# An eleventh weight place from halved attention maps, weight loads three places ahead, and a moved second-tile key projection

## The chip, the cores and the metric

One NeuronCore of a Trainium2 chip. The time is the device time of the kernel in microseconds, the median of the runs of one program.

## The reference, cut to what matters

A two-layer encoder over 256 tokens of width 1024, in float32, taken as two tiles of 128 tokens. For each layer `mix = token_mixers(h)`, then `h = layer_norm(a*h + mix)`, then the experts, then a gate:

```python
proj = h @ w_in                  # dq, dk, dv (differential attention), sq, sk, sv (sparse attention), iq, ik, iw (indexer)
w = a[:, 0] - lam * a[:, 1]      # 4 heads, two softmax maps each
_, sel = lax.top_k(iscore, 64)   # sparse attention: 8 heads, one map each, over the 64 chosen keys
q = (xt @ w_q).reshape(TOKEN_BLOCK, 8, 2, 128)           # PEER
s = jnp.einsum('thcd,hckd->thck', q, skf)                # top 16 of each half, top 16 of the 256 sums
act = jax.nn.gelu(jnp.einsum('thkd,td->thk', u_tab[eidx], xt))
out = jnp.einsum('thk,thkd->td', g * act, v_tab[eidx])   # 128 experts of a token
r = r + sigmoid(r @ ple_wg + ple_bg) * (p @ ple_wp)
```

Attention is causal in chunks of 64: tile 0 sees 128 keys, tile 1 sees 256.

## The kernel before

**Passes and pairs.** Each of the four (layer, tile) combinations is a pass: MIX[0..3] mixes the tokens and chooses experts, then 128 indirect gathers bring for each token one row of u and v (128 x 2048 float32, 1 MB a gather), then CLOSE[0..3] applies the gate. The gathers of a pass are worked off in 64 pairs, which make up a phase: phase 1 works off the experts of pass 0 and, woven in between the pairs, runs MIX[1]; phase 2 runs CLOSE[0] and MIX[2], phase 3 CLOSE[1] and MIX[3], phase 4 CLOSE[2] and the start of CLOSE[3]. Phase 0, ahead of them, has MIX[0] and the beginning of MIX[1] and no pairs.

**A pair.** GpSimd issues the gathers into a ring of 8 row slots (L622), each after TensorE has used the slot's former row. VectorE makes the dot product with the token (L1303), ScalarE the gelu and the scaled diagonal matrix `dg` (L832, L835), TensorE adds the weighted v rows into PSUM (`acc`, L1663, in the last pass L1658), which frees the two slots.

**Weights.** They come in blocks of 128 x 2048 (1 MB) from SyncE's queue (L571), strictly in the order in which TensorE uses them, into a `store` of 10 places; a load waits until the last reader of its place is done. `count_uses` gives each block the place that has been free longest. MIX[n] of tile 1 uses the weights of the same layer as MIX[n-1]: eight blocks (`KEPT_BLOCKS`: the sub-keys and all expert-query blocks but the first) stay in the store from tile 0 to tile 1. For MIX[1] six further blocks (`EARLY`: the index weights, dq0, dq1, dk0, dk1) are put by MIX[0] into ring slots 2 to 7, and the first gathers into those slots wait until MIX[1] has used them (the wait on `block_done` ahead of L622). dq1 stands for the second half of the differential-query weights, dk0 and dk1 for those of the keys, pq2a and pq2b for the expert queries of group 2, ps2 for their scores against the sub-keys.

**Order.** It is written out by hand. `START_PE`, `START_ACT`, `START_DVE` list phase 0 (a + marks parts of MIX[1]); `FIRST_PLAN`, `PROJECT_PLAN`, `ATTEND_PLAN`, `CLOSE_PLAN` give for each part the pair ahead of which TensorE, ScalarE and VectorE run it; `attend_first` and `attend_last` shift the plan in phases 1 and 3, `behind_close` in phase 2. `SINGLY_FIRST` and `SINGLY_PROJECT` place the projections of MIX[1] and MIX[3] one block a pair. The selection of experts is in steps A (top 16 of the two halves), B (top 16 of the sums) and C (looking up the indices) for five groups of heads: A2a is step A of group 2, first head. They run on VectorE (`choose`, from L1227), with an exponential on ScalarE (L777) in step C.

**Maps.** `ex` (128 x 8 x 256) holds the eight exponential maps of either attention, then the key scores of all 16 expert lists and the lookup's one-hot rows; `probsT` (128 x 16 x 128) their transposes, the expert queries, and the gains and shifts of the closing norm. The part `wts0`/`wts1` combines the two differential maps (from L993); `spt0`, `spt1` and `spv` transpose the sparse maps and multiply them with the values (L1480).

## Time and profile before

| | |
|---|---|
| median of 3 runs | 1598.83 us (1597.42 to 1599.74) |
| profiled execution, its own time | 1597.55 us |
| span of its instructions | 1595.8 us |
| TensorE, VectorE, ScalarE, GpSimd busy | 76%, 66%, 42%, 36% |
| moved | 648.45 MB, 406 GB/s over the span |
| indirect gathers | 510, median 16.0 us from issue to landing |
| weight loads of 1 MB into the store | 93, median about 10 us from issue to landing |
| chain that ended last | DMA 45%, TensorE 30%, VectorE 14%, ScalarE 7% |

How to read it: the page cuts the span into 40 slices of 39.9 us and gives for each the busy tenths of each engine and the GB/s moved; a window view gives the same for stretches one names. A wait is put down to the instruction that came last among those waited for. Times of single instructions come from the timeline view, which merges neighbours of one line.

### The profile page before, as it was taken

Reading aid. Unit: us, or ns where it says so; the run is one execution under the profiler, and the core shown is the slowest. Engines: PE = TensorE matmul, PEld = TensorE weight load, DVE = VectorE, ACT = ScalarE, POOL = GpSimd, SP = SyncE. Lnnn points to the kernel's source line nnn. Section 1 sums busy time; section 2 is a strip of 40 time slices with the busy share of each in tenths; the row PEclk is TensorE's granted clock in tenths of the full one; section 3 lists DMA queues with packets and bytes.
Section 4 is the critical chain, followed back from the end, with each engine's and each line's share of the span. In section 5 each row is a group of like instructions: output and inputs, shape, how many; then the busy total and the mean of one; then the engine's idle time right before and its main releaser. Section 6 shows DMA issues by size and latency. Waiting matters only on the chain.

```text
span 1595.8 us, 22703 instructions
## 1 busy us (share of the span) xinstructions
PE 1213.1 (76%) x8234; PEld 603.9 (38%) x8234; DVE 1045.3 (66%) x2636; ACT 668.6 (42%) x2027; POOL 580.9 (36%) x518
## 2 busy tenths in 40 slices
PE   9999868787868689786895977978798768444556
PEld 9686423333532266231551335524255223000112
DVE  3467997745778664654688684575578958644555
ACT  2323445723344435363344532536344534323444
POOL 0013443443333323343344332334443434544441
PEclk9999989898888899797997978999899876555557
DMA  9869999999999999999999999999999999999996
GB/s 384 360 250 396 396 421 420 421 421 420 421 420 421 417 396 421 421 420 421 421 421 421 421 417 370 420 421 420 422 420 419 420 421 420 422 421 421 421 421 248
DMA packets 91344, 648.45 MB, mean 406 GB/s; under 512 B 10144, under 2 KB 11616, under 8 KB 13152
## 3 DMA queue, kind: packets, MB, share of 16 engines
q0 software_dynamic: 74016, 536.90, 81.3%
q1 hardware_dynamic: 16704, 109.76, 16.8%
q8 instruction: 65, 1.06, 0.3%
q10 hardware_dynamic: 512, 0.34, 0.1%
q14 instruction: 47, 0.39, 0.1%
HBM read 645.91 MB, written 1.05 MB: 405 GB/s over the span
## 4 chain that ended last, share of the span: by engine, by line
DMA 45%; PE 30%; DVE 14%; ACT 7%; issue 3%; POOL 2%; SPq 0%; ACTq 0%; DVEq 0%; POOLq 0%
DMA rows<-uv_dram,rows_of 39%; PE bank L1343 10%; PE acc L1663 7%; DVE rows L1303 7%; PE bank L1361 5%; DMA store<-wmix_dram 4%; POOL rows L622 2%; ACT dg L835 1%; PE acc L1658 1%; ACT L832 1%; ACT ex L748 1%; PE bank L1614 1%; DMA rows<-wmix_dram 1%; ACT gel L832 1%; DMA store<-wclose_dram 1%
## 5 line engine op out<-in xcount | busy, mean ns | idle before, releaser
L622 POOL DMA_INDIRECT rows<-uv_dram,rows_of x510 | 576.7, 1131 | 985.9 <-PE acc L1663 661.3
L1303 DVE CUSTOM_DVE_ANT_0 rows<-rows,hb 128x1024 f32<-128x1024 f32 x384 | 463.9, 1224 | 313.1 <-DMA rows<-uv_dram,rows_of 310.6
L1663 PE MATMUL acc<-rows,dg 64*64 64x512 f32 x3072 | 453.1, 701 | 198.0 <-ACT dg L835 196.2
L832 ACT ACTIVATE gel<-dots 128x1 f32<-128x1 f32 x512 | 102.7, 201 | 630.1 <-DVE dots L1303 628.7
L1663 PEld LDWEIGHTS acc<-rows,dg 64*64 64x64 f32 x3072 | 102.0, 145 | 459.7 <-ACT dg L835 369.3
L1343 PE MATMUL bank<-xT,store 128*128 128x128 f32 x1888 | 235.1, 286 | 15.7 <-DMA store<-wmix_dram 10.4
L1343 PEld LDWEIGHTS bank<-xT,store 128*128 128x128 f32 x1888 | 225.5, 200 | 55.5 <-issue 41.9
L1303 DVE CUSTOM_DVE_ANT_0 rows<-rows,store 128x1024 f32<-128x1024 f32 x128 | 155.5, 1224 | 119.3 <-DMA rows<-uv_dram,rows_of 118.7
L1658 PE MATMUL acc<-rows,dg 128*32 128x256 f32 x1024 | 119.7, 565 | 133.3 <-ACT dg L835 132.8
L835 ACT ACTIVATE dg<-dg,gel 128x64 f32<-128x64 f32 (+1 forms) x512 | 174.7, 341 | 48.4 <-ACT gel L832 1.5
L1361 PE MATMUL bank<-store,xT 128*128 128x512 f32 x352 | 166.3, 618 | 17.2 <-DMA store<-wmix_dram 14.4
L829 ACT ACTIVATE dg<-fixed,g_of 128x64 f32<-128x64 f32 (+1 forms) x512 | 143.5, 329 | 1.4 <-ACT probsT L648 0.3
L1658 PEld LDWEIGHTS acc<-rows,dg 128*32 128x32 f32 x1024 | 25.9, 132 | 222.9 <-ACT dg L835 212.5
L1361 PEld LDWEIGHTS bank<-store,xT 128*128 128x128 f32 x352 | 66.3, 196 | 110.4 <-issue 94.0
L832 ACT ACT_TABLE_LOAD x51 | 65.4, 1283 | 0.9
L648 ACT ACTIVATE probsT<-bank 128x512 f32<-128x512 f32 (+1 forms) x59 | 30.7, 545 | 42.4 <-PE bank L1343 32.6
L1303 DVE DVE_READ_ACCUMULATOR2_ANT dots<- 128x1 f32 x512 | 42.1, 82 | 0.0
L648 ACT ACTIVATE qT<-bank 128x512 f32<-128x512 f32 (+1 forms) x18 | 9.9, 550 | 59.7 <-PE bank L1343 49.8
L1489 PE MATMUL bank<-prm,fixed 64*128 64x256 f32 x96 | 27.5, 433 | 0.0
L777 ACT ACT_TABLE_LOAD x20 | 25.7, 1283 | 0.4
L1253 DVE TENSOR_TENSOR ex<-ex,i16f 128x512 f32<-128x512 f32 (+1 forms) x38 | 22.6, 594 | 1.3
L1256 DVE TENSOR_REDUCE sel<-ex 128x32 f32<-128x512 f32 (+1 forms) x38 | 22.4, 588 | 1.3
(230 smaller groups left out, 1016.2 us busy)
## 6 DMA issues: line engine op xcount, KB each, us to landing
store<-wmix_dram SPq DMA_DIRECT2D x78, 1024.0 KB, 9.7
store<-wclose_dram SPq DMA_DIRECT2D x15, 1024.0 KB, 10.4
rows<-uv_dram,rows_of POOLq DMA_INDIRECT x510, 16.0
rows<-wmix_dram SPq DMA_DIRECT2D x5, 1024.0 KB, 14.8
...
```

The source lines that it names most:

```text
L622: pool.indirect_dma_start(out=rows[:, slot, :], out_offset=None, in_=uv_d[phase // TILES], in_offset=bass.IndirectOffsetOnAxis(ap=rows_of[ ...
L648: ins = A(out, src, func)
L777: A(gexp[:, 0:gs], gexp[:, 0:gs], ACT.Exp).then_inc(gexp_ready, 1)
L829: A(dg[:, s + j, 0:w], one, ACT.Identity, scale=g_of[:, phase % 2, col:col + 1]).then_inc(diag_ready, 1)
L832: A(gel[:, s + j:s + j + 1], dots[:, s + j:s + j + 1], ACT.Gelu).then_inc(gelu_done, 1)
L835: A(dg[:, s + j, 0:w], dg[:, s + j, 0:w], ACT.Identity, scale=gel[:, s + j:s + j + 1]).then_inc(dg_ready, 1)
L1303: V.tensor_tensor_reduce(out=rows[:, s, 0:D], in0=rows[:, s, 0:D], in1=tokens, scale=1.0, scalar=0.0, op0=ALU.mult, op1=ALU.add, accum_out ...
L1343: ins = MM(bk[:, T * at:T * at + T], w[:, T * c:T * c + T], src[:, c, :], start=(c == 0), stop=(c == KC - 1))
L1361: ins = MM(bk[:], xT[:, 2 * q + c, :], w[:, 512 * c:512 * c + 512], start=(q == 0 and c == 0 and extra is None), stop=(q == 3 and c == 1), ...
L1489: ins = MM(bk[:, QCOLS * j:QCOLS * j + QCOLS], chooser(first + i // 2, 2 * (i % 2) + j), prm[:], start=True, stop=True)
L1658: ins = MM(quarters(acc, c)[BT * k:BT * k + BT, :], dg[:, s, 0:BT], rows[:, s, D + 256 * k:D + 256 * k + 256], start=False, stop=False, sk ...
L1663: ins = MM(acc[HT * j:HT * j + HT, 512 * r:512 * r + 512], dg[at, s, :], rows[at, s, D + 512 * j:D + 512 * j + 512], start=False, stop=Fal ...
```

## The change

- `ex` and `probsT` are halved. For tile 1 the eight maps go through in two halves of four: the second half's exponentials wait until the first half has been combined (differential) or transposed (sparse); `wts` and `spv` are split accordingly; the scores of groups 3 and 4 are copied once earlier groups are looked up. The gains and shifts of the closing norm lie half in `sc`.
- The store has 11 places.
- A block of MIX[1] and later takes the third newest of the free places; MIX[0]'s blocks take the oldest, as before. The places for the last pass's spread tokens are the three longest free then, no longer 0, 1 and 2.
- dk0 and dk1 of MIX[0] are loaded into the store and held there for MIX[1] (`LENT`), no longer into ring slots 6 and 7. MIX[1] runs them ahead of pairs 3 and 9 of phase 1, no longer in phase 0; the rest of its projections moves by four pairs.
- The selections of pass 0 in phase 1 and their queries are moved by one to three pairs, and `ATTEND_PLAN` by up to two, `attend_first` by up to two more.

```diff
@@ -46,7 +46,7 @@
-PLACES = 10
+PLACES = 11
...
+HELD = 4
...
@@ -157,7 +158,7 @@
-        blocks = [b for b in blocks if b not in EARLY]
+        blocks = [b for b in blocks if b not in EARLY + LENT]
...
@@ -169,23 +170,23 @@
...
-    ("exps0", None, 18, None), ("exps1", None, 19, None), ("dv0", 17, None, None), ("dv1", 18, 19, None),
+    ("exps0", None, 18, None), ("dv0", 17, None, None), ("dv1", 18, 19, None),
...
-    ("sel0", None, None, 20), ("wts0", None, None, 21), ("wts1", None, None, 22), ("sel1", None, None, 22),
+    ("wts0", None, None, 20), ("exps1", None, 21, None), ("sel0", None, None, 21), ("wts1", None, None, 22), ("sel1", None, None, 22),
...
-    ("sexp0", None, 26, None), ("sexp1", None, 27, None), ("rms", None, 28, 27), ("rms2", None, None, 29),
-    ("spt0", 27, 28, None), ("spt1", 28, 29, None), ("spv", 30, None, None), ("merge", None, None, 32),
-    ("gb0", 28, 29, None), ("gb1", 29, 30, None), ("mT0", 30, 31, None), ("mix0a", 32, None, None),
-    ("mT1", 33, 34, None), ("mix1a", 33, None, None), ("mix0b", 34, None, None), ("mix1b", 35, None, None),
+    ("sexp0", None, 26, None), ("rms", None, 28, 27), ("rms2", None, None, 29),
+    ("spt0", 27, 28, None), ("sexp1", None, 28, None), ("gb0", 28, 29, None), ("spv0", 29, None, None), ("spt1", 30, 31, None),
+    ("gb1", 31, 32, None), ("mT0", 31, 32, None), ("spv1", 32, None, None), ("mix0a", 33, None, None), ("mix1a", 34, None, None),
+    ("merge", None, None, 34), ("mT1", 35, 36, None), ("mix0b", 36, None, None), ("mix1b", 37, None, None),
...
-    ("B1a", None, None, 49), ("perm0", 49, None, 51), ("pq3b", 49, 50, None), ("C1a", None, 51, 50), ("ps3", 50, 51, None),
+    ("B1a", None, None, 49), ("perm0", 49, None, 51), ("pq3b", 49, 50, None), ("C1a", None, 51, 50), ("ps3", 51, 53, None),
...
-    ("A2a", None, None, 53), ("A2b", None, None, 54), ("ps4", 54, 55, None), ("B2a", None, None, 56), ("B2b", None, None, 57),
-    ("C2a", None, 59, 58), ("C2b", None, None, 60), ("perm2", 61, None, 63), ("A3a", None, None, 61), ("A3b", None, None, 62),
+    ("A2a", None, None, 53), ("A2b", None, None, 54), ("B2a", None, None, 56), ("B2b", None, None, 57),
+    ("C2a", None, 59, 58), ("ps4", 58, 61, None), ("C2b", None, None, 60), ("perm2", 61, None, 63), ("A3a", None, None, 61), ("A3b", None, None, 62),
...
@@ -220,20 +221,20 @@
-START_PE = ("wake T idx dq0 dq1 dk0 dk1 iw ds0 ix sq0 sq1 dv0 dv1 dpt sk0 dpv sk1 ss0 sv0 sv1 mT0 mix0a spt0 spt1 mix1p spv mix1a mT1 "
-            "T1+ mix0b mix1b idxa+ h1T pq0a ps0 idxb+ dq0+ pq1a init ps1 dq1+ dk0+ dk1+").split()
+START_PE = ("wake T idx dq0 dq1 dk0 dk1 iw ds0 ix sq0 sq1 dv0 dv1 dpt sk0 dpv sk1 ss0 sv0 sv1 mT0 mix0a spt0 spt1 mix1p spv0 spv1 mix1a mT1 "
+            "T1+ mix0b mix1b idxa+ h1T pq0a ps0 idxb+ dq0+ pq1a init ps1 dq1+").split()
...
-    ("pq2a", 0, None, None), ("pq2b", 1, 2, None), ("pq3a", 2, None, None), ("ps2", 3, 4, None), ("pq3b", 4, 5, None),
-    ("pq4a", 5, None, None), ("ps3", 6, 7, None), ("pq4b", 7, 8, None), ("ps4", 9, 10, None),
+    ("pq2a", 1, None, None), ("pq2b", 2, 3, None), ("ps2", 4, 5, None), ("pq3a", 5, None, None), ("pq3b", 7, 8, None),
+    ("ps3", 8, 9, None), ("pq4a", 10, None, None), ("pq4b", 11, 12, None), ("ps4", 13, 14, None),
...
-    ("A2a", None, None, 4), ("A2b", None, None, 5), ("B2a", None, None, 6), ("B2b", None, None, 7), ("C2a", None, 9, 8),
-    ("C2b", None, None, 9), ("perm2", 9, None, 11), ("A3a", None, None, 11), ("A3b", None, None, 12), ("B3a", None, None, 13),
-    ("B3b", None, None, 14), ("C3a", None, 16, 15), ("C3b", None, None, 16), ("perm3", 17, None, 19), ("A4a", None, None, 17),
-    ("A4b", None, None, 18), ("B4a", None, None, 19), ("B4b", None, None, 20), ("C4a", None, 22, 21), ("C4b", None, None, 22),
-    ("perm4", 23, None, 25),
+    ("A2a", None, None, 5), ("A2b", None, None, 6), ("B2a", None, None, 7), ("B2b", None, None, 8), ("C2a", None, 10, 9),
+    ("C2b", None, None, 10), ("perm2", 10, None, 12), ("A3a", None, None, 12), ("A3b", None, None, 13), ("B3a", None, None, 14),
+    ("B3b", None, None, 16), ("C3a", None, 18, 17), ("C3b", None, None, 18), ("perm3", 18, None, 20), ("A4a", None, None, 19),
+    ("A4b", None, None, 20), ("B4a", None, None, 21), ("B4b", None, None, 23), ("C4a", None, 25, 24), ("C4b", None, None, 25),
+    ("perm4", 26, None, 28),
...
@@ -242,8 +243,18 @@
     ("dk0", 16, None, None), ("dk1", 17, 18, None), ("iw", 18, 19, None), ("sq0", 18, None, None), ("sq1", 19, 20, None),
 ]
 SINGLY_FIRST = [
-    ("T", 9, 10, None), ("par", 9, 10, None), ("sq0", 11, None, None), ("iw", 13, 14, None), ("sq1", 13, 14, None),
+    ("dk0", 3, None, None), ("dk1", 9, 10, None), ("T", 13, 14, None), ("par", 13, 14, None), ("sq0", 15, None, None),
+    ("iw", 17, 18, None), ("sq1", 17, 18, None),
 ]
+def behind_mix(row):
...
+    part, *pairs = row
+    late = [p for p in pairs if p is not None]
+    if part[:2] in ("sp", "gb", "mT", "mi", "me") or min(late) < 37:
+        return row
+    return (part, *(None if p is None else p + (2 if p < 54 else 1 if p < 62 else 0) for p in pairs))
...
 SINGLY = {"dv0": (18, None, None), "dv1": (19, 20, None), "sv0": (20, None, None), "sv1": (21, 22, None)}
...
@@ -257,12 +268,15 @@
...
 def attend_first(p):
...
-    return p + max(0, min(6, 6 - (p - 50) // 3))
+    return p + max(0, min(8, 8 - (p - 50) // 3))
...
+ATTEND_PLAN = [behind_mix(row) for row in ATTEND_PLAN]
...
 def make_plan():
@@ -270,7 +284,6 @@
-    plan["ACT"][1].append((1, "dk1", MIX[1]))
...
@@ -318,18 +331,18 @@
...
-EARLY = [(U_IQ, U_IQ + 1), (U_IK,)] + [tuple(units_of(part)) for part in ("dq0", "dq1", "dk0", "dk1")]
-EARLY_SLOTS = (3, 2, 4, 5, 6, 7)
+EARLY = [(U_IQ, U_IQ + 1), (U_IK,)] + [tuple(units_of(part)) for part in ("dq0", "dq1")]
+EARLY_SLOTS = (3, 2, 4, 5)
+LENT = [tuple(units_of(part)) for part in ("dk0", "dk1")]
...
-HX_BLOCKS, SPREAD_BLOCK = 2, 2
-HELD_LATE = (0, 1, SPREAD_BLOCK)
+AHEAD = 3
...
-    if run is MIX[1] and block in EARLY:
+    if run is MIX[1] and block in EARLY + LENT:
...
@@ -348,7 +361,7 @@
...
-    uses, free = [0] * PLACES, [-1] * PLACES
+    uses, free, late = [0] * PLACES, [-1] * PLACES, ()
...
@@ -357,8 +370,10 @@
             if run is MIX[0] and block in EARLY:
                 place = (PLACES + EARLY.index(block), 0)
             else:
-                at = min((a for a in range(PLACES) if run is not CLOSE[2] or a not in HELD_LATE), key=lambda a: free[a])
-                assert free[at] < i
+                if run is CLOSE[2] and not late:
+                    late = tuple(sorted(range(PLACES), key=lambda a: free[a])[:3])
+                open_to = sorted((a for a in range(PLACES) if free[a] < i and a not in late), key=lambda a: free[a])
+                at = open_to[0] if run is MIX[0] else open_to[max(0, len(open_to) - AHEAD)]
                 place = (at, uses[at])
                 uses[at] += 1
                 free[at] = end if run is CLOSE[2] else last[run.key, block]
@@ -369,11 +384,12 @@
...
-    return bank, unit, uses
+    return bank, unit, late, uses
...
-BANK, UNIT, USES = count_uses()
+BANK, UNIT, HELD_LATE, USES = count_uses()
+SPREAD_BLOCK = HELD_LATE[0]
...
@@ -416,8 +431,8 @@
-        ex = sb("ex", [128, 8, SEQ])
-        probsT = sb("probsT", [128, 16, T])
+        ex = sb("ex", [128, HELD, SEQ])
+        probsT = sb("probsT", [128, 2 * HELD, T])
...
@@ -500,6 +519,16 @@
+        def map_of(run, i):
...
+            i = i % HELD if run.tile else i
+            return ex[:].rearrange("p a k -> p (a k)")[:, run.keys * i:run.keys * i + run.keys]
...
+        def halves_of(h0, nh):
...
+            at = 2 * (h0 % HELD)
+            return slice(at, at + 2 * nh)
...
@@ -732,8 +763,10 @@
                 if part in ("exps0", "exps1"):
...
+                    if half and tile:
+                        act.wait_ge(dw_ready, DIFF_HEADS * n + DIFF_HEADS // 2)
...
-                        A(ex[:, i, 0:run.keys], sc[:, i, 0:run.keys], ACT.Exp, bias=nmx[:, i:i + 1], scale=SCALE,
+                        A(map_of(run, i), sc[:, i, 0:run.keys], ACT.Exp, bias=nmx[:, i:i + 1], scale=SCALE,
...
@@ -744,12 +777,14 @@
                 if part in ("sexp0", "sexp1"):
...
+                    if half and tile:
+                        act.wait_ge(*full_at(run, "spt1"))
...
-                        A(ex[:, i, 0:run.keys], sc[:, i, 0:run.keys], ACT.Exp, bias=snmx[:, i:i + 1], scale=SCALE,
+                        A(map_of(run, i), sc[:, i, 0:run.keys], ACT.Exp, bias=snmx[:, i:i + 1], scale=SCALE,
...
-                        take(run, name, quarter(probsT, int(name[3])))
+                        take(run, name, quarter(probsT, int(name[3]) % 2))
...
@@ -769,7 +804,9 @@
...
-                    take(run, part[:3], lists[:, 2 * h0:2 * h0 + 2 * nh, :].rearrange("p c t -> p (c t)"), slice(0, 2 * nh * T))
+                    if part in ("ps3", "ps4"):
+                        act.wait_ge(*((rows_picked, len(GROUPS) * n + g - 1) if n < LAST else (chosen_ready, g - 1)))
+                    take(run, part[:3], lists[:, halves_of(h0, nh), :].rearrange("p c t -> p (c t)"), slice(0, 2 * nh * T))
...
@@ -990,24 +1027,26 @@
...
+                    half = int(part[3])
+                    if half == 0:
...
+                    maps = slice(4 * half, 4 * half + 4)
+                    dve.wait_ge(dexp_ready, 8 * n + 4 * half + 4)
...
@@ -1466,20 +1506,23 @@
...
+                if part in ("spv0", "spv1"):
...
-                    bk, full = bank(run, "spv")
...
+                    bk, full = bank(run, "spv") if half == 0 else opened(run, "spv")
...
+                            ins = MM(bk[:, DH * hd:DH * hd + DH], probsT[:, ((tile + 1) * hd + k) % (2 * HELD), :],
...
```

## Rows read from the trace of the kernel before

**Rows 1.** The page: its head, the 40 slices' rate, the packets.

```profile
span 1595.8 us, 22703 instructions
...
GB/s 384 360 250 396 396 421 420 421 421 420 421 420 421 417 396 421 421 420 421 421 421 421 421 417 370 420 421 420 422 420 419 420 421 420 422 421 421 421 421 248
DMA packets 91344, 648.45 MB, mean 406 GB/s; under 512 B 10144, under 2 KB 11616, under 8 KB 13152
```

**Rows 2.** Windows: length, PE, PEld, DVE, ACT, POOL busy, granted clock, DMA share, GB/s.

```profile
70.00:105.00 35.00, 33.56 (x210) 25.40 (x209) 12.54 (x45) 5.38 (x12) 2.12 (x2) 1.00 0.50 170
105.00:115.00 10.00, 10.00 (x89) 9.07 (x88) 9.16 (x37) 5.15 (x11) 3.89 (x5) 1.00 0.95 368
...
125.00:145.00 20.00, 19.86 (x167) 13.53 (x166) 12.36 (x44) 9.66 (x26) 7.69 (x9) 1.00 0.97 370
...
160.00:175.00 15.00, 11.60 (x89) 4.70 (x87) 14.55 (x40) 10.45 (x29) 8.05 (x7) 0.96 0.93 350
175.00:550.00 375.00, 283.80 (x1728) 129.06 (x1724) 271.23 (x712) 162.14 (x484) 139.99 (x126) 0.88 1.01 421
550.00:585.00 35.00, 25.32 (x167) 13.60 (x168) 31.26 (x70) 16.30 (x46) 11.82 (x11) 0.80 0.99 386
...
950.00:970.00 20.00, 12.02 (x93) 9.09 (x93) 15.91 (x37) 9.83 (x28) 5.30 (x4) 0.81 1.00 408
970.00:985.00 15.00, 15.00 (x122) 11.91 (x123) 4.93 (x8) 3.31 (x13) 4.79 (x4) 0.91 0.75 289
```

**Rows 3.** SyncE's timeline, 90 to 100 and 175 to 185: start, length.

```profile
96.49 0.33 SPq L571 DMA_DIRECT2D store<-wmix_dram  x1
...
180.33 0.33 SPq L571 DMA_DIRECT2D store<-wmix_dram  x1
```

**Rows 4.** TensorE's timeline, 96 to 130.

```profile
108.08 10.88 PE L1343 MATMUL bank<-res,rows 128*128 128x128 f32 x96
118.80 3.74 PE L1343 MATMUL bank<-xT,store 128*128 128x128 f32 x32
122.46 1.95 PE L1663 MATMUL acc<-rows,dg 64*64 64x512 f32 x16
```

**Rows 5.** GpSimd's timeline, 100 to 130: in brackets idle before, releaser.

```profile
112.09 0.93 POOL L622 DMA_INDIRECT rows<-uv_dram,rows_of  x1 [3.22 <-PE bank L1343]
...
119.23 0.93 POOL L622 DMA_INDIRECT rows<-uv_dram,rows_of  x1 [2.64 <-PE bank L1343]
124.36 0.94 POOL L622 DMA_INDIRECT rows<-uv_dram,rows_of  x1 [4.20 <-PE acc L1663]
```

**Rows 6.** ScalarE's and VectorE's timelines, 112 to 132.

```profile
115.06 0.35 ACT L835 ACTIVATE dg<-dg,gel 128x64 f32<-128x64 f32 x1
...
120.61 1.22 DVE L1303 CUSTOM_DVE_ANT_0 rows<-rows,hb 128x1024 f32<-128x1024 f32 x1
...
130.37 0.17 DVE L1278 TENSOR_REDUCE gsum<-gexp 128x1 f32<-128x16 f32 x1 [7.07 <-ACT gexp L777]
```

**Rows 7.** TensorE's timeline, 950 to 980.

```profile
957.47 1.95 PE L1663 MATMUL acc<-rows,dg 64*64 64x512 f32 x16
967.40 6.31 PE L1343 MATMUL bank<-xT,store 128*128 128x128 f32 x32 [7.98 <-DMA store<-wmix_dram]
973.65 1.95 PE L1663 MATMUL acc<-rows,dg 64*64 64x512 f32 x16
```

**Rows 8.** SyncE's timeline, 955 to 958.

```profile
957.57 0.80 SPq L571 DMA_DIRECT2D store<-wmix_dram  x2
```

**Rows 9.** TensorE's timeline, 574 to 592.

```profile
574.46 5.62 PE L1343 MATMUL bank<-xT,store 128*128 128x128 f32 x48 [1.36 <-ACT xT L648]
...
581.89 7.41 PE L1343 MATMUL bank<-xT,store 128*128 128x128 f32 x64
```

**Rows 10.** The chain of waits at 337, and the window 335 to 350 around it.

```profile
337.62 10.24 DMA store<-wmix_dram
...
335.00:350.00 15.00, 12.12 (x52) 4.32 (x51) 4.93 (x8) 3.73 (x15) 3.75 (x4) 1.00 1.02 422
```

More of the change, by code:

```diff
@@ L811, in spread_out @@
                 for half, name in enumerate(banks_of(run, f"hx{c}")):
-                    take(run, name, hx[:, c, 512 * half:512 * half + 512])
+                    take(run, name, hx_of(c)[:, 512 * half:512 * half + 512])
                 for name in banks_of(run, f"hx{c}"):
@@ L992, in part_of @@
                     ins.then_inc(iscore_ready, 1)
[L993 to L995 removed]
+                if part in ("wts0", "wts1"):
+                    half = int(part[3])
+                    if half == 0:
+                        dve.wait_ge(lamexp_ready, n + 1)
+                        V.tensor_tensor(lamw[:, 4:5], lamw[:, 3:4], lamw[:, 2:3], ALU.subtract).then_inc(L.sem, L.one())
+                        settle()
+                        V.tensor_scalar(lamw[:, 5:6], lamw[:, 4:5], -LAM_INIT[run.layer], None, ALU.add).then_inc(L.sem, L.one())
+                    maps = slice(4 * half, 4 * half + 4)
+                    dve.wait_ge(dexp_ready, 8 * n + 4 * half + 4)
+                    V.reciprocal(rden[:, maps], den[:, maps]).then_inc(L.sem, L.one())
@@ L996, in part_of @@
                     settle()
-                    V.tensor_scalar(lamw[:, 5:6], lamw[:, 4:5], -LAM_INIT[run.layer], None, ALU.add).then_inc(L.sem, L.one())
-                    dve.wait_ge(dexp_ready, 8 * (n + 1))
-                    V.reciprocal(rden[:], den[:]).then_inc(L.sem, L.one())
+                    V.tensor_scalar(nmx[:, maps], rden[:, maps], lamw[:, 5:6], None, ALU.mult).then_inc(L.sem, L.one())
                     settle()
-                    V.tensor_scalar(nmx[:], rden[:], lamw[:, 5:6], None, ALU.mult).then_inc(L.sem, L.one())
+                    for hd in (2 * half, 2 * half + 1):
+                        V.tensor_scalar(map_of(run, 2 * hd + 1), map_of(run, 2 * hd + 1), nmx[:, 2 * hd + 1:2 * hd + 2],
+                                        None, ALU.mult).then_inc(L.sem, L.one())
@@ L1002, in part_of @@
                     settle()
-                    for hd in range(DIFF_HEADS):
-                        V.tensor_scalar(ex[:, 2 * hd + 1, 0:nk], ex[:, 2 * hd + 1, 0:nk], nmx[:, 2 * hd + 1:2 * hd + 2],
-                                        None, ALU.mult).then_inc(L.sem, L.one())
-                if part == "wts1":
-                    settle()
-                    for hd in range(DIFF_HEADS):
-                        V.scalar_tensor_tensor(sc[:, hd, 0:nk], ex[:, 2 * hd, 0:nk], rden[:, 2 * hd:2 * hd + 1],
-                                               ex[:, 2 * hd + 1, 0:nk], ALU.mult, ALU.add).then_inc(dw_ready, 1)
+                    for hd in (2 * half, 2 * half + 1):
+                        V.scalar_tensor_tensor(sc[:, hd, 0:nk], map_of(run, 2 * hd), rden[:, 2 * hd:2 * hd + 1],
+                                               map_of(run, 2 * hd + 1), ALU.mult, ALU.add).then_inc(dw_ready, 1)
```

42 lines of the change are left out of this document (22 added, 20 removed).

## The prediction

> **What bounds the kernel now.** The page comes first [rows 1]. The program moves 648.45 MB; its best slices move 420 to 422 GB/s and most slices stand there. At 421 GB/s that is 1540.2 us of a span of 1595.8 us, so the 16 DMA engines are the bound and only some 55 us are theirs to lose. TensorE (76%) and VectorE (66%) matter only where they keep a transfer from being asked for. So I read the trace as a list of holes: in a stretch of T us at g GB/s, T x (1 - g/421) us are lost. The windows [rows 2] give 20.9 us in 70 to 105; 1.3 in 105 to 115; 2.4 in 125 to 145; 2.5 in 160 to 175; 2.9 in 550 to 585; 0.6 + 4.7 in 950 to 985; most of the rest lies in the first 70 us and in the tail. Between 175 and 550 the rate is 421, as in nearly all later slices. An edit that neither closes nor opens a hole moves nothing: bytes are the same before and after the change.
>
> Then each hole's cause. *70 to 105*: no expert is chosen before 102.6 us, so only weights can move, and the places for them are full: SyncE issues a load at 96.49 and none again until 180.33 [rows 3]. *125 to 145*: TensorE runs six blocks of column weights (three of them, dq1, dk0 and dk1 of the second tile, in the 10.88 us row, then pq2a) before the first pair at 122.46 [rows 4]. The gathers into row slots 5, 6 and 7 wait one by one for dq1, dk0 and dk1, and the one into slot 0 again for that pair [rows 5]; VectorE meanwhile waits 7.07 us for an exponential which ScalarE makes only behind the copies of dk1 and pq2b [rows 6]. *970 to 985*: TensorE ends a pair at 959.4 and the next at 975.6, 16.2 us later, since dq0 was still under way [rows 7]. Its load and dq1's were issued from 957.57 on, within 0.8 us [rows 8], once the index weights were used: eight of the ten places hold weights kept for this tile, two circulate. The eight row slots are 8 x 2.49 = 19.9 us of transfer (1 MB at 421 GB/s), half of it spent when the stall began, so the engines ran dry at 970.
>
> **The change, part by part.** *The loan of dk0 and dk1.* Rows slots 6 and 7 are free for gathers at once; of eleven places the loan holds two, so nine circulate up to the first gather where ten did. One load fewer is under way before 105: 1 MB, 2.5 us more of the first hole. **Lost: 2.5.**
>
> *dk0 and dk1 behind pairs 2 and 8, pq2a behind pair 0.* The first pair no longer waits for 10.88 x 2/3 + 3.7 = 10.9 us of TensorE; its factors are there by 115.4 [rows 6], so it ends near 117.3 instead of 124.4, and slots 0 and 1 are asked for then. The gathers of slots 6 and 7 go out right behind slot 5's (112.09, 0.94 us each and a short gap), the last near 114.6 against 119.23. By 117.3, 9 MB are asked for and some 5 moved (3.7 in 105 to 115, and 2.3 us at the full rate), so about 10 us are in hand, until 127; pair 1 has its dot products at 121.8 [rows 6] and ends near 124.5, still inside. The copy of pq2b moves behind the exponential, so most of the 7.07 us goes. The hole of 125 to 145 closes: **2.4 gained**. That of 105 to 115 stays (it is the latency of the first gathers and slot 5's wait for dq1, which nothing moves).
>
> *Selections spread.* The same VectorE work, with more pairs that carry none (3, 4, 11, 15, 22; before only 3 and 10). In 160 to 175 VectorE is busy 14.55 of 15 us: the slots come free late because of it. With the 7 us from above in hand, and with two weight loads (behind dk0 and dk1) that now fall into a stretch without any [rows 3], I take 2.0 of the 2.5. **Gained: 2.0** (bounds 0 and 2.5).
>
> *Eleventh place in the fourth pass.* Three places circulate: the index weights and dq0 are there before the index part. dq1 and dk0 then take the two loads of 957.57, land near 967.3 [rows 7, 8] and dq1 is wanted at about 965.2 (957.5 + pair 1.95 + block 3.8 + pair 1.95). A wait of 2.1 us instead of 9.8, with two more gathers asked for at 965. The 5.3 us of 950 to 985 shrink to the 0.6 that VectorE causes. **Gained: 4.7** (bounds 2.4, half, and 5.3).
>
> *Loads three places ahead.* A load now goes into the third newest free place, not the oldest. In the first pass the oldest is still taken, and in the second and fourth only three places circulate anyway, so it bites in the third, where up to ten loads ran ahead. There TensorE is in one piece from 574 to 643: index part, pair, two blocks (7.4 us), pair, at 9.3 us a pair [rows 9]. dq1's load is issued when the first index block is done, at about 578.3, and wanted at 585.7; if it takes 9.8 us like that of rows 7, TensorE waits 2.4 us there. The hole that opens is bounded by nothing (337.62: a wait of 10.24 us for a load, at 422 GB/s all the while [rows 10]) and by that of rows 7 (4.7). The engines are at 386 GB/s just before, thus with little queued, and I take 1.2, the lower quarter. **Lost: 1.2.**
>
> *Halved maps.* The second half of the exponentials waits for the first half's weights or transposes, each placed a pair or more earlier on its engine; ps3 and ps4 copies wait for a lookup one pair back. Queued behind each such wait on ScalarE are the diagonals of the next pair, for which TensorE waits. The cover is the eight-deep ring; if it were gone, one wait would cost a pair, 5 us. The split products add two reciprocals and two small products a pass, each like the 0.17 us row of rows 6, under transfers. The rest of the mixer moves two pairs later; its first choices stand two pairs ahead of the gather that reads them, even in the pass where they are latest. **Nothing.**
>
> Sum against the profiled execution, 1597.55 us (span 1595.8 and 1.75 around it): -2.5 + 2.4 + 2.0 + 4.7 - 1.2 = 5.4 gained, 1592.15. The median shown is 1598.83, 1.28 above that execution, so for a median 1598.83 - 5.4 = **1593.4**.
>
> **The rivals.** *(a) More closes.* If no wait in the third pass opens a hole, and its 550 to 585 hole (2.9, VectorE busy 31.26 of 35 us) is filled since loads that ran ahead now come later: 2.4 + 2.5 + 5.3 + 2.9 + 1.3 - 2.5 = 11.9, 1586.9. For it, lost time is where loads are missing; against, a load still starts only when a block is used, and none is used there.
>
> *(b) The loads set the pace.* In rows 8 two loads, 2 MB, with gathers outstanding, took 9.8 us until TensorE went on: one MB per 4.9 us, while TensorE uses one per 4.65 in the third pass (9.3 a pair). Ten loads in hand hide that; three don't. At 2 x 4.98 = 9.96 us a pair, seven pairs last 4.6 us longer; if that reaches the end, 5.4 - 4.6 = 0.8 gained, 1598.0. Against: while TensorE waits, loads and gathers keep the engines at 421. The Trainium skill's page DMA: Bandwidth & Descriptors (Queues, rings and completion order) has each DMA engine take turns between the queue rows that have work; by that rule loads get half of the rate while gathers are queued, and the sum would be this 1598.0. Rows 8 fit it.
>
> *(c) Slower: starved third pass.* If three of its seven double blocks find a load late enough that two pair ends stand over 16.2 us apart (the gap of rows 7, from which a hole opened), each costs 4.7: 14.1 lost against 5.4 + 1.2 gained, 1598.83 + 7.5 = 1606.3. For: lead falls from ten loads to three in the densest stretch. Against: it takes 7 us of lateness on top of 9.3, three times, with three loads outstanding; rows 10 show ten us of lateness for nothing.
>
> *(d) The place is eaten by the loan.* The start gains nothing (0 of 2.0, 1.0 of 2.4) and the fourth pass half: -2.5 + 1.0 + 2.4 - 1.2 = -0.3, 1599.1.
>
> **How the numbers follow.** Forecast 0.60, (a) 0.13, (b) 0.07, (c) 0.10, (d) 0.10. A measurement of this kernel can tell about 0.2%, 3.2 us, from no change. Faster: forecast nearly whole (0.58) and (a) 0.13, 0.71. Same: (b), (d) and the forecast's upper edge, 0.18. Slower: (c) and 0.01 for sizes, 0.11. The range runs from (a) 1586.5 to 1600, past (b) and (d); outside are (c) and a twentieth beyond the ends. The bounds of the unknown terms (2.0, 2.3 and 3.5 downwards, 0.5, 0.6 and 1.2 upwards) lie within it but for all bad ones at once.
>
> **What would show it.** Right: first pair's matmuls near 115 and row slot 0 asked for again near 117; 125 to 145 and 160 to 175 at 415 GB/s or more; 70 to 105 poorer, near 140 GB/s; no DMA wait of TensorE over 3 us after the last pass's index part and no slice there at 370; a wait of 2 to 3 us for dq1 in the third pass. Wrong: new slices under 410 in the third pass (c), a VectorE hole that moved rather than closed, or 70 to 105 unchanged.

## The result, and the profile after

The kernel after takes 1600.39 us (median of 20 runs, 1597.35 to 1605.05) against 1597.66 us (20 runs, 1595.52 to 1600.56) of the kernel before on the same chip: a ratio of 1.0016, interval [1.0009, 1.0023]. It is slower by 2.7 us. That is less than the 0.2% that the prediction called tellable, but the interval leaves out a ratio of 1. The forecast was 5.4 us faster. The profiled execution of after took 1601.31 us.

The page of after: its head, the rate in the 40 slices, the packets.

```profile
span 1599.5 us, 22715 instructions
...
GB/s 385 333 255 421 420 421 405 421 421 421 421 420 389 403 407 420 421 421 422 421 420 421 421 420 420 421 421 409 421 421 394 387 421 420 422 421 421 421 421 248
DMA packets 91344, 648.45 MB, mean 405 GB/s; under 512 B 10144, under 2 KB 11616, under 8 KB 13152
```

Against [rows 1] the same bytes moved. The slices 4, 5 and 25 (396, 396, 370 before) now stand at 421, 420 and 420. New weak slices are the 7th, 13th, 14th, 28th, 31st and 32nd. The windows of after, first the stretches of [rows 2], then those that are new (columns as there):

```profile
0.00:70.00 70.00, 64.94 (x453) 54.25 (x454) 30.16 (x110) 21.60 (x59) 0.20 (x4) 1.00 0.97 390
70.00:105.00 35.00, 33.56 (x210) 25.56 (x209) 12.70 (x46) 5.38 (x12) 2.17 (x2) 1.00 0.44 162
105.00:115.00 10.00, 6.89 (x62) 5.76 (x64) 9.15 (x37) 5.15 (x11) 5.26 (x7) 1.00 0.97 380
125.00:145.00 20.00, 18.81 (x158) 12.41 (x156) 14.77 (x49) 8.05 (x27) 7.65 (x8) 1.00 1.01 420
160.00:175.00 15.00, 15.00 (x132) 11.91 (x135) 11.37 (x27) 7.57 (x21) 5.73 (x6) 1.00 1.01 418
250.00:265.00 15.00, 15.00 (x97) 10.21 (x95) 12.97 (x30) 6.08 (x18) 5.26 (x4) 0.89 0.98 378
485.00:500.00 15.00, 15.00 (x56) 5.58 (x55) 14.41 (x36) 5.19 (x15) 3.48 (x4) 0.87 0.85 332
550.00:585.00 35.00, 31.85 (x252) 23.78 (x252) 19.88 (x40) 11.82 (x37) 9.04 (x8) 0.95 0.99 386
950.00:970.00 20.00, 18.62 (x144) 13.04 (x140) 18.76 (x42) 10.48 (x31) 8.60 (x8) 0.93 1.01 418
970.00:985.00 15.00, 14.10 (x121) 11.13 (x122) 3.70 (x6) 3.53 (x13) 4.82 (x5) 1.00 1.02 422
1095.00:1110.00 15.00, 15.00 (x100) 7.35 (x100) 7.54 (x13) 9.36 (x30) 7.54 (x7) 0.84 0.96 384
1235.00:1245.00 10.00, 8.76 (x39) 2.52 (x40) 9.59 (x29) 4.24 (x14) 3.41 (x4) 0.83 0.70 262
1245.00:1265.00 20.00, 15.01 (x130) 5.96 (x128) 19.31 (x62) 12.06 (x31) 7.25 (x7) 0.91 0.99 377
```

With the prediction's measure, T x (1 - g/421), both executions can be put into one account. The kernel before ran at 400 GB/s in 0 to 70 and at 419 to 422 in each of the five stretches further on that are new here.

| stretch | before, us lost | after | gained | forecast |
|---|---|---|---|---|
| 0 to 115 | 3.5 + 20.9 + 1.3 = 25.7 | 5.2 + 21.5 + 1.0 = 27.7 | -2.0 | -2.5 |
| 125 to 145 | 2.4 | 0 | 2.4 | 2.4 |
| 160 to 175 | 2.5 | 0.1 | 2.4 | 2.0 |
| 550 to 585 | 2.9 | 2.9 | 0 | -1.2 |
| 950 to 985 | 5.3 | 0.1 | 5.2 | 4.7 |
| 250 to 265 | 0 | 1.5 | -1.5 | 0 |
| 485 to 500 | 0 | 3.2 | -3.2 | 0 |
| 1095 to 1110 | 0 | 1.3 | -1.3 | 0 |
| 1235 to 1265 | 0.1 | 3.8 + 2.1 = 5.9 | -5.8 | 0 |
| sum | | | -3.8 | 5.4 |

The spans differ by 3.7 us, so the account of these two executions closes. Its first row depends on the execution: experiments 8 and 12, which start as the kernel before does, lost 27.2 us up to 115, where the table has 25.7; the kernel after and the six experiments with its loan lost 27.7 to 27.9. The five stretches that the forecast priced gave 8.0 us; four that it priced at nothing took 11.8. Half of that lies in one place near 1235. There TensorE, VectorE and GpSimd of after read (timelines, in brackets idle before and releaser):

```profile
1227.17 0.44 PE L1580 MATMUL bank<-chosen,fixed 128*32 128x8 f32 x32
1227.54 3.84 PE L1383 MATMUL bank<-xT,store 128*128 128x128 f32 x32
1236.24 3.63 PE L1706 MATMUL acc<-rows,dg 64*64 64x512 f32 x16 [4.86 <-ACT dg L872]
...
1220.43 1.23 DVE L1343 CUSTOM_DVE_ANT_0 rows<-rows,hb 128x1024 f32<-128x1024 f32 x1 [0.64 <-DMA rows<-uv_dram,rows_of]
1227.69 0.17 DVE L1137 CAST rows_of<-bank 128x16 uint32<-128x16 f32 x1 [6.02 <-PE bank L1580]
1234.29 1.22 DVE L1343 CUSTOM_DVE_ANT_0 rows<-rows,hb 128x1024 f32<-128x1024 f32 x1
...
1227.93 0.94 POOL L651 DMA_INDIRECT rows<-uv_dram,rows_of  x1 [0.30 <-issue]
1238.53 0.94 POOL L651 DMA_INDIRECT rows<-uv_dram,rows_of  x1 [9.67 <-PE acc L1706]
```

`perm1` spreads the chosen experts of one group: TensorE multiplies (L1580), VectorE takes the result (L1137). In the third phase the kernel before has TensorE do it ahead of pair 57 and VectorE take it ahead of pair 59. In the kernel after `behind_mix` moves TensorE's row (53) by two and VectorE's (55) by one, and `attend_last`, which gives a row a smaller addition the later its pair, brings both to 59. VectorE works ahead of TensorE, so it stands still for 6.02 us with a pair's dot products behind it. Then it makes A2a and A2b, both on pair 59 too (6.6 us from 1227.69 to 1234.29), before the two dot products. TensorE has no factors, no pair ends, no row slot comes free, and GpSimd asks for nothing for 9.67 us. The next gap is 5.73 us, to 1251.55: VectorE makes B2b and C2a, both on pair 61, from 1241.84 to 1247.61, and TensorE waits 3.03 us for that pair's factors. Meanwhile the transfers run out.

### The profile page after: what moved, and what is told of

Same layout as the page of the kernel before. It is cut to its first block, busy times and chain, and to the rows that moved or that the text cites. A ratio compares the mean times of both kernels' runs of the same rounds, so it can differ in the third digit from the quotient of the medians.

```text
span 1599.5 us, 22715 instructions
## 1 busy us (share of the span) xinstructions
PE 1211.1 (76%) x8234; PEld 605.7 (38%) x8234; DVE 1047.0 (65%) x2644; ACT 664.3 (42%) x2024; POOL 573.6 (36%) x518
## 4 chain that ended last, share of the span: by engine, by line
DMA 40%; PE 31%; DVE 18%; ACT 6%; issue 3%; POOL 2%; SPq 0%; POOLq 0%; ACTq 0%; DVEq 0%
DMA rows<-uv_dram,rows_of 36%; PE bank L1383 9%; PE acc L1706 9%; DVE rows L1343 8%; PE bank L1401 6%; POOL rows L651 2%; DMA store<-wmix_dram 2%; DMA qT<-pT_dram 1%; PE acc L1701 1%; ACT dg L872 1%; PE bank L1631 1%; ACT L869 1%; DVE i L942 1%; DVE i L933 1%; PE bank L1657 1%
## 5 line engine op out<-in xcount | busy, mean ns | idle before, releaser
L651 POOL DMA_INDIRECT rows<-uv_dram,rows_of x510 | 568.6, 1115 | 996.6 <-PE acc L1706 680.9
L1706 PE MATMUL acc<-rows,dg 64*64 64x512 f32 x3072 | 445.2, 689 | 207.7 <-ACT dg L872 206.3
L1383 PE MATMUL bank<-xT,store 128*128 128x128 f32 x1952 | 239.8, 283 | 13.6 <-DVE sc L1005 7.6
L1383 PEld LDWEIGHTS bank<-xT,store 128*128 128x128 f32 x1952 | 229.4, 197 | 52.4 <-issue 33.7
L677 ACT ACTIVATE probsT<-bank 128x512 f32<-128x512 f32 (+1 forms) x53 | 27.7, 542 | 49.1 <-PE bank L1383 37.7
L677 ACT ACTIVATE val<-bank 128x512 f32<-128x512 f32 x16 | 9.4, 593 | 41.8 <-PE bank L1401 24.9
L814 ACT ACT_TABLE_LOAD x20 | 25.7, 1283 | 0.4
L1570 PEld LDWEIGHTS bank<-store,probsT 128*128 128x128 f32 x128 | 17.5, 208 | 17.4 <-issue 13.4
## 6 DMA issues: line engine op xcount, KB each, us to landing
store<-wmix_dram SPq DMA_DIRECT2D x80, 1024.0 KB, 10.3
```

What stands on the lines that cost most here:

```text
L651: pool.indirect_dma_start(out=rows[:, slot, :], out_offset=None, in_=uv_d[phase // TILES], in_offset=bass.IndirectOffsetOnAxis(ap=rows_of[ ...
L677: ins = A(out, src, func)
L814: A(gexp[:, 0:gs], gexp[:, 0:gs], ACT.Exp).then_inc(gexp_ready, 1)
L1383: ins = MM(bk[:, T * at:T * at + T], w[:, T * c:T * c + T], src[:, c, :], start=(c == 0), stop=(c == KC - 1))
L1706: ins = MM(acc[HT * j:HT * j + HT, 512 * r:512 * r + 512], dg[at, s, :], rows[at, s, D + 512 * j:D + 512 * j + 512], start=False, stop=Fal ...
```

## The experiments

Each ratio is to the kernel before, run on the same chip beside the experiment; the kernel after has 1.0016. What is lost in a stretch is read from one execution of each kernel.

Theories after that reading. The shared pair: the hole of 1235 comes from `perm1` on the same pair on both engines. The places: it, and the hole of 485, come from where the loads are put, with the closing blocks' loads late. The bunching: both come from selection steps that the uneven shift put on one pair. The loan: places lost to it cost the start.

**1 and 2. The places.** A closing block, then every block, takes the oldest free place.

```diff
-                at = open_to[0] if run is MIX[0] else open_to[max(0, len(open_to) - AHEAD)]
+                at = open_to[0] if run is MIX[0] or run.stage == "close" else open_to[max(0, len(open_to) - AHEAD)]
```

In the second the line is `at = open_to[0]`.

> The changed kernel, but blocks of the closing stage (gate and ple weights) take the place that has been free longest; only the mixer's keep the third newest. Theory L (late gate load: the first closing block waits for the place of the sub-keys, which the moved score part of group 4 reads last, and the gate's pT load stands behind it): the wait of TensorE for pT at the second phase's start goes (9.7 us) and with it the hole at 485 to 500, 3.2 us; about 1597 against 1600.4. Theory S (bunched selections hold the slots back there): the hole stays, 1600 to 1601.

> The changed kernel with the oldest free place for every block, loads as far ahead as places allow. Theory L: as with the closing blocks alone, about 1597. Theory P (loads that ran ahead filled the stretches in which VectorE is the bound, so with a lead of three those stretches became holes): also the holes of 550 to 585 and 1235 to 1265 shrink, 1592 to 1594. If the short lead was worth something in the mixer: above the kernel with only the closing blocks on the oldest place.

Measured: 1605.59 us, ratio 1.0047 [1.0034, 1.0060], and 1603.51 us, 1.0035 [1.0022, 1.0048]. Neither gained. In the kernel after, TensorE waits 9.68 us at 484.31 for `qT`, whose load stands behind the first closing block's; in the first experiment that wait is gone and 490 to 510 still loses 3.3 us. The second settles more. With every block in the oldest place, 485 to 550 runs at 420 GB/s, with the selections as bunched as before. The kernel after's wait and gap, then 490 to 495 of after and of the second experiment:

```profile
484.31 5.89 PE L1657 MATMUL bank<-store,qT 128*128 128x512 f32 x8 [9.68 <-DMA qT<-pT_dram]
...
491.53 0.94 POOL L651 DMA_INDIRECT rows<-uv_dram,rows_of  x1 [14.97 <-PE acc L1706]
...
490.00:495.00 5.00, 5.00 (x26) 2.16 (x26) 4.72 (x15) 4.37 (x14) 1.88 (x2) 1.00 0.79 267
...
490.00:495.00 5.00, 4.54 (x28) 1.85 (x27) 4.96 (x10) 3.77 (x10) 2.09 (x2) 1.00 1.01 418
```

By the kernel's own placing, the first closing block of the kernel after goes into the place that `ps3` reads last, ahead of pair 60 of the first phase; with the oldest place it goes into one last read ahead of pair 44. So the places do open the hole of 485. In the first experiment the wait is gone but the mixer's loads are still held back: 485 to 510 moves 0.91 MB of plain loads, in the second 3.57 MB, and VectorE is busy 48.24 of the 50 us from 500 on. At the third phase's end it is otherwise. Though the closing block for the last phase is asked for at 1184.60, no longer at 1246.58, the hole near 1240 grows, from 5.9 to 10.1 us. VectorE's wait for `perm1` grew with it:

```profile
1233.60 0.17 DVE L1137 CAST rows_of<-bank 128x16 uint32<-128x16 f32 x1 [7.03 <-remote]
```

TensorE's `perm` is at 1231.15 there and done by 1231.59; what holds VectorE for the last 2 us of the wait the profile gives only as `remote`, and so it is in the other runs that wait 7 us or more. The second experiment has a wait of 7.00 us and loses 10.6 us. So an earlier load helps nothing there.

**3 and 4. The bunching.** The shift behind the mixer's end becomes two pairs below 52 and one below 56; then this with the first experiment's edit.

```diff
-    return (part, *(None if p is None else p + (2 if p < 54 else 1 if p < 62 else 0) for p in pairs))
+    return (part, *(None if p is None else p + (2 if p < 52 else 1 if p < 56 else 0) for p in pairs))
```

> The changed kernel with the selection steps shifted by 2 up to pair 51 and by 1 up to 55 instead of 2 up to 53 and 1 up to 61, so that in the third and fourth pass no two A or B steps of a group fall on one pair except where the shift of phase 1 or 3 puts them. Theory S: the hole of 1235 to 1265 (5.8 us) shrinks to 2 or less, 1596 to 1597. Theory L alone: nothing at 1235, 1600 to 1601.

> Both of the edits (closing blocks on the oldest place, selection steps less bunched). Theories L and S together: 3.2 and about 4 us gone, 1593 to 1594, below both kernels. If the two holes have one cause, no more than the better of the two alone.

Measured: 1599.13 us, 1.0008 [0.9999, 1.0017], and 1600.56 us, 1.0015 [1.0006, 1.0024]. The hole of 1235 to 1265 falls to 3.0 and 3.2 us, those near 490 (3.3, 4.8) and 560 stay. The edit also parts `perm1`, to pair 58 on TensorE and 59 on VectorE, whose wait for it goes from 6.02 to 0.35 us (`perm0` now waits 1.30). And it moves bunches more than it dissolves them: C1a and C1b share pair 57, A2b and B2a pair 59, with 6.5 us from the take of `perm1` to the next dot product. So the uneven shift is a part of the hole, but this experiment tests neither theory alone.

**5. The shared pair.** One number: VectorE's take of `perm1` three pairs later in the plan.

```diff
-    ("C1b", None, None, 52), ("pq4a", 52, None, None), ("perm1", 53, None, 55), ("pq4b", 53, 54, None),
+    ("C1b", None, None, 52), ("pq4a", 52, None, None), ("perm1", 53, None, 58), ("pq4b", 53, 54, None),
```

> The changed kernel with one number moved: VectorE takes over the permuted rows of group 1 in the last pass (perm1) ahead of pair 61 instead of 59; TensorE still makes them ahead of pair 59. In the changed kernel both stand at pair 59 and VectorE, which runs ahead of TensorE, stood still some 5 to 7 us for them before it did both top-16 steps of group 2. Theory Q (that wait opens the hole of 1235 to 1265): the hole falls from 5.9 us to 3 or less, 1597.5. Theory S (only the two steps on one pair matter): the hole stays at 5 to 6, 1600.

Measured: 1597.16 us (before 1598.39), 0.9997 [0.9988, 1.0006], no longer slower than the kernel before. The same stretch, TensorE's and GpSimd's timelines, then the windows:

```profile
1224.49 0.44 PE L1580 MATMUL bank<-chosen,fixed 128*32 128x8 f32 x32
...
1230.96 1.95 PE L1706 MATMUL acc<-rows,dg 64*64 64x512 f32 x16 [1.69 <-ACT dg L872]
...
1232.35 0.96 POOL L651 DMA_INDIRECT rows<-uv_dram,rows_of  x1 [6.17 <-PE acc L1706]
```

```profile
1235.00:1245.00 10.00, 7.70 (x45) 2.73 (x38) 9.69 (x22) 4.20 (x10) 3.16 (x3) 0.89 0.99 409
1245.00:1265.00 20.00, 13.97 (x144) 5.70 (x144) 19.02 (x67) 12.60 (x38) 10.32 (x9) 0.97 1.01 420
```

VectorE waits for no `perm`. GpSimd's gap is 6.17 us instead of 9.67 and what is left of the hole is 0.3 us in 1235 to 1245, although A2a and A2b still share pair 59. The shared pair is the largest single cause of the slowdown: the ratios differ by 0.19%, some 3 us. The execution read here is the fastest of the eleven, so its holes make the gain look larger.

**6. The first phase as before.** Projections, selections and `attend_first` of the first phase as in the kernel before (the removed lines of the diff ahead of the prediction), dk0 and dk1 at pairs 3 and 9 as after.

> The changed kernel with the first phase's selections, the second tile's T to sq1 and the shift of phase 1 (6 instead of 8 pairs) as before; dk0 and dk1 stay in the store and at pairs 3 and 9. Theory F (the spread pushes the second tile's selections into the closing work at the phase boundary): the hole of 485 to 500 (3.2 us) goes, that of 550 to 570 stays; a hole near 160 of up to 2.4 may come back. 1598 to 1600. Theory E (the early start alone closes 125 to 175): no hole near 160, 1597.

Measured: 1602.0 us, 1.0022 [1.0012, 1.0031]. 125 to 145 and 160 to 175 run at 422 and 421 GB/s, with the selections not spread. So dk0 and dk1 out of phase 0 close both holes; the spreading is not needed there. 485 to 500 is at 421 too, and 250 to 265 at 424: the holes of 485 and 250 need the spread first phase. `ps3` is read two pairs earlier here, the closing block is asked for at 457.49 instead of 471.92, and TensorE has no wait for `qT`. With experiment 2, the hole of 485 takes both: a reader moved back and a rule that gives the closing block the place of this reader. But 535 to 605 loses 6.2 us and 1235 to 1275 7.8, so the run gains nothing.

**7. No loan.** dk0 and dk1 of MIX[1] back in ring slots 6 and 7 and in phase 0, the rest as after.

```diff
-EARLY = [(U_IQ, U_IQ + 1), (U_IK,)] + [tuple(units_of(part)) for part in ("dq0", "dq1")]
-EARLY_SLOTS = (3, 2, 4, 5)
-LENT = [tuple(units_of(part)) for part in ("dk0", "dk1")]
+EARLY = [(U_IQ, U_IQ + 1), (U_IK,)] + [tuple(units_of(part)) for part in ("dq0", "dq1", "dk0", "dk1")]
+EARLY_SLOTS = (3, 2, 4, 5, 6, 7)
+LENT = []
```

> The changed kernel without the loan: dk0 and dk1 go into ring slots 6 and 7 and are used before the first pair, as before. Prediction's account: idle time of 60 to 115 falls by 2.5 us per extra place under way (two places back: 24.2 less 2.5 to 5), and the hole of 125 to 145 (2.4 us) returns: between 1598 and 1600.5. If the loan was worth its price: above 1600.4.

Measured: 1597.63 us, 0.9997 [0.9988, 1.0006]. Its windows:

```profile
0.00:70.00 70.00, 66.30 (x453) 55.70 (x454) 30.06 (x110) 21.60 (x59) 0.20 (x4) 1.00 0.98 400
70.00:105.00 35.00, 33.56 (x209) 25.47 (x208) 12.70 (x45) 5.38 (x12) 2.07 (x2) 1.00 0.55 200
125.00:145.00 20.00, 18.32 (x154) 10.73 (x152) 16.05 (x54) 9.11 (x30) 11.60 (x10) 1.00 1.02 423
...
1235.00:1245.00 10.00, 10.00 (x45) 3.42 (x46) 9.49 (x30) 3.69 (x12) 4.16 (x4) 0.78 0.62 223
```

Eleven places without the loan lose 3.5 + 18.4 us up to 105, with it 5.2 + 21.5: two places cost 4.8 us, 2.4 each, the forecast's 2.5 for one. Over all executions the start varies: up to 115 the four runs without the loan lose 23.0 to 24.5 us, the seven with it 27.7 to 27.9, so two places cost 3.2 to 5.0. And 125 to 145 stays full with dk0 and dk1 in phase 0, where pq2a behind pair 0, the spread selections and the eleventh place remain. So the loan bought nothing that its removal would take back. The later hole grew instead (223 GB/s; 7.9 us in 1230 to 1265; VectorE's wait for `perm` 7.67 us, GpSimd's gap 11.52).

**8. The kernel before with the third newest place**, and its ten places.

> The kernel before with one edit: blocks of the second and later passes take the third newest free place (with ten places). Prediction's account: one more hole of about 1.2 us where the third pass's dq1 comes late, 1599 to 1600 against 1598. Theory N (a short lead opens nothing by itself, the engines have the outstanding loads): same as before within 1 us. Theory H (short lead helps): the hole of 555 to 585 shrinks.

Measured: 1597.97 us, 0.9998 [0.9989, 1.0007]; 950 to 985 still loses (405 and 336 GB/s). Loads three places ahead neither cost nor give in this kernel, whose `ps3` is ahead of pair 56; 485 to 500 is at 422. It is the eleventh place that fills the fourth pass.

**9 to 12.** The two largest causes removed together; this with experiment 3's shift; this with the steps of the first and third phase written out one to a pair and the oldest place everywhere; and the shared pair put into the kernel before (`perm1` at 53 for both engines, which `attend_last` brings to 57 and 57).

```diff
-    ("C1b", None, None, 52), ("pq4a", 52, None, None), ("perm1", 53, None, 55), ("pq4b", 53, 54, None),
+    ("C1b", None, None, 52), ("pq4a", 52, None, None), ("perm1", 53, None, 53), ("pq4b", 53, 54, None),
```

That is the twelfth; of the eleventh, the positions of some steps in the third phase (TensorE, ScalarE, VectorE):

```diff
+    3: {"C1a": (None, 58, 57), "C1b": (None, None, 58), "perm1": (60, None, 62), "A2a": (None, None, 59), "A2b": (None, None, 60),
+        "B2a": (None, None, 61), "B2b": (None, None, 62), "C2a": (None, 64, 63), "C2b": (None, None, 64), "ps4": (62, 65, None),
```

> The changed kernel with the second tile's differential keys back in ring places in the first phase, and VectorE's take of perm1 three pairs later. If the loan and perm1's pair are two separate costs: idle DMA of about 19.6 us in 60-115 (not 24.2) and none in 1235-1265 (not 5.9), so a span of about 1591 to 1593 and a time of 1592 to 1594. Rival, what is gained at the start is given back by a later hole (as in the run without the loan alone, where 1230-1265 grew to 7.9): 1596 to 1598.

> The one before with the steps behind the mixer's end unbunched as well (two pairs later only below 52, one only below 56). If the idle time between the phases (1.6 at 250, 3.2 at 485, 2.8 at 550) comes of steps bunched on a pair: as the one before less 0 to 1 us, 1591 to 1594. Rival, the closing half arrives too late for perm1 or ps4, now earlier on TensorE: holes near 500 and 1240 of 3 to 5 us each, 1596 to 1600.

> The same with the first and third phase's selections spread to one step a pair, and each load into the oldest free place again. If bunched steps of VectorE make the holes at 485, 550 and 1100: these fall from 3.2, 2.8 and 1.2 us to under 1 each, and the time is 1588 to 1592. Rival, the holes are not VectorE's but come of loads whose place is read late: they stay, 1594 to 1598, and the spread adds nothing.

> The kernel before with VectorE's take of perm1 two pairs earlier, on the pair on which TensorE makes it (57), as the changed kernel has it (59 and 59). If the shared pair alone stops VectorE: a wait of VectorE for perm of 3 to 7 us near 1215, idle DMA of 2 to 6 us near 1220-1250 where the kernel before has none, and 1600 to 1604. Rival, it needs the halved steps beside it (A2a and A2b on the same pair): no hole there, 1597 to 1599.

Measured, against 1597.39 us of the kernel before: 1593.58 us, 0.9972 [0.9963, 0.9982]; 1594.87 us, 0.9982 [0.9973, 0.9991]; 1591.23 us, 0.9958 [0.9944, 0.9972]; 1597.19 us, 0.9994 [0.9986, 1.0003].

The ninth holds what was expected: 60 to 115 loses 20.9 us (19.6 expected), next to nothing is left near 1235, and two edits turn 2.7 us slower into 3.8 us faster. The tenth gives no more: 485 to 495 loses 4.0 us, where TensorE waits 7.89 us for `qT`. The eleventh is the fastest; its intervals overlap with the ninth's, so the last 2 us are likely, not certain. Its windows show what is left of the holes:

```profile
485.00:500.00 15.00, 15.00 (x71) 6.22 (x64) 14.52 (x39) 9.56 (x23) 6.69 (x6) 1.00 1.01 419
550.00:585.00 35.00, 31.61 (x233) 20.40 (x230) 30.44 (x88) 16.15 (x49) 15.08 (x12) 0.83 1.01 420
1235.00:1245.00 10.00, 8.62 (x48) 3.24 (x48) 9.48 (x25) 5.27 (x16) 3.88 (x4) 1.00 1.01 420
```

The holes of 485 and 550 are gone, though that of 1100 (1.6 us) stays and 1015 to 1030 loses 2.3. The edit changed places too. For 485 that is enough by experiment 2, so nothing here shows that bunched steps had made it. For 550 experiment 2 lost 3.8 us with the places alone, so there the steps, or both together, count.

The twelfth is the miss that teaches most. VectorE's, GpSimd's and SyncE's timelines of it, then a window:

```profile
1219.54 0.17 DVE L1098 CAST rows_of<-bank 128x16 uint32<-128x16 f32 x1 [4.42 <-PE bank L1537]
1223.04 1.22 DVE L1303 CUSTOM_DVE_ANT_0 rows<-rows,hb 128x1024 f32<-128x1024 f32 x1
...
1226.39 0.94 POOL L622 DMA_INDIRECT rows<-uv_dram,rows_of  x1 [9.45 <-PE acc L1663]
...
1219.50 0.44 SPq L571 DMA_DIRECT2D store<-wclose_dram  x1
```

```profile
1225.00:1235.00 10.00, 6.08 (x40) 1.80 (x40) 9.62 (x35) 3.61 (x13) 3.74 (x4) 0.84 1.02 419
```

The wait is there as the theory has it (4.42 us), GpSimd's gap is nearly after's (9.45), and no hole opens. Two things differ next to it: one selection step follows the take, not two (3.5 us to the next dot product against 6.6), and three loads (332 KB, 1 MB, 128 KB) are issued within the gap, 1.5 MB or 3.6 us at the full rate. The kernel before has these loads in the same place and nearly the same gap, without any wait for `perm`:

```profile
1219.59 0.43 SPq L571 DMA_DIRECT2D store<-wclose_dram  x1
...
1224.65 0.94 POOL L622 DMA_INDIRECT rows<-uv_dram,rows_of  x1 [7.98 <-PE acc L1663]
```

So the shared pair lengthened that gap by only 1.5 us. In the kernel after the closing block comes at 1246.58, behind the gap. The end of the third phase in ten runs:

| run | VectorE waits for `perm1` | longest gap of gathers | lost in 1230 to 1275 |
|---|---|---|---|
| before | none | 8.0, with 3.6 us of loads in it | 0.2 |
| 12, kernel before, shared pair | 4.4 | 9.5, with 3.6 us of loads in it | 0.3 |
| 5, take three pairs later | none | 6.2 | 0.7 |
| 3, unbunched | 0.4 | 5.2 | 3.1 |
| 4, unbunched, closing blocks oldest | 0.4 | 5.2 | 3.2 |
| after | 6.0 | 9.7 | 5.8 |
| 6, first phase as before | 7.7 | 11.6 | 7.8 |
| 7, no loan | 7.7 | 11.5 | 7.9 |
| 1, closing blocks oldest | 7.0 | 11.6 | 10.1 |
| 2, all blocks oldest | 7.0 | 11.6 | 10.6 |

So the shared pair is what its removal in 5 shows it to be, a necessary part of the kernel after's hole, but by 12 it is not sufficient. The second selection step behind it and the loads outside the gap are the likely rest; neither was tried alone, and the two kernels differ in more than these. The length of the gap does not rank the losses by itself, as 3 and 4 show.

## Why the prediction was wrong

*The method held.* The bound is DMA, the bytes are the same, and the difference of the two executions followed the holes to 0.1 us.

*Loan, first pair, fourth pass: right.* The start lost 2.0 (2.5 forecast), though against the starts of experiments 8 and 12 it would be 0.5: the sign holds, the size is not pinned. The first pair's matmuls are at 114.87, slot 0 was asked for at 116.77, and 125 to 145 runs at 420 GB/s. One reason in it was too narrow: experiment 7 shows dk0 and dk1 had no need to leave phase 0. In the fourth pass the eleventh place did what was worked out, to the wait:

```profile
970.90 3.84 PE L1383 MATMUL bank<-xT,store 128*128 128x128 f32 x32 [2.28 <-DMA store<-wmix_dram]
```

2.28 us for dq1 where 2.1 stood in the working and 7.98 in [rows 7]. Gained 5.2, forecast 4.7.

*Selections spread: right sum, wrong cause.* 160 to 175 gained 2.4, but experiment 6 has it without the spreading, by the earlier start. The sum is in part luck: in experiment 12, whose first phase is that of the kernel before, the stretch lost only 0.4 (410 GB/s). And the spreading had a price that the prediction left out, the holes of 250 and 485.

*Three places ahead: priced in the wrong phase.* In the third pass 1.2 lost were forecast, 0 came. TensorE's longest wait for a load in 570 to 645 is 1.56 us (at 571.68), and 550 to 585 is at 386 GB/s as before (with VectorE busy 19.88 us in place of 31.26, so it is not the same hole left alone). At the second phase's start, which the prediction did not look at, the rule gave the first closing block the place of the late `ps3`: 9.68 us of TensorE, 3.2 us of the engines. Rivals (b) and (c) fell with the forecast of 1.2: the pairs of the third pass are no further apart for want of loads. The Trainium skill's page DMA: Bandwidth & Descriptors (Queues, rings and completion order) states the taking of turns, packet by packet; that loads would get half of the rate by it was the prediction's own step. Its cost did not come in the third pass: the loads' median is 10.3 us from issue to landing, and it stays hidden. Ahead of 485 a load's lateness does show: from 472 to 484, with loads and gathers outstanding, plain loads moved 1.79 of 5.03 MB, and the closing blocks took 16.4 us (median) from issue to landing.

*Halved maps and the moved mixer: the step that failed.* The prediction says "The rest of the mixer moves two pairs later; its first choices stand two pairs ahead of the gather that reads them", and so "**Nothing.**" It looked at the one reader outside the mixer and took the move as rigid. It is not rigid: it is 2, 1 or 0 pairs by threshold, and the phase's own mapping shrinks it again. Written out pair by pair for each engine it would have shown `perm1` on pair 59 for TensorE and VectorE, A2a and A2b with it, B2b with C2a on 61, A3a with A3b on 64. The prediction had counted ten us of transfers in hand elsewhere, and here the gathers stop for 9.67 us. In place of nothing the runs show 5.8 us near 1235, closed to 0.7 by moving the one take (experiment 5). The two other holes that it priced at nothing, 3.2 near 485 and 1.5 near 250, need the spread first phase (experiment 6), and that of 485 the late place as well (experiment 2); what stops the engines near 250 stays open. The halved maps themselves have one stretch to answer for: ScalarE has the scale of the norm, the copy of `spt0` and the second exponentials all on pair 33 (before, the exponentials were on 32), TensorE then waits 4.06 us for `dg`, up to 1094.86, and 1095 to 1110 loses 1.3 us. That is read off the plan and the timelines, not tried.

*The rivals.* None had this mechanism. (d) came nearest in time (1599.1), by a wrong way: the start and the fourth pass gave all they were to give. The slower rival looked for the danger in late loads of the third pass, where three were to cost 4.7 us each; one late load did cost, at the start of the second phase, and the larger price lay in the order that the change rewrites.
